# A long convolution's tap stage in row pairs, its transforms on three bank pairs, and a router loop in another order

## The reference, cut to what matters

```
h = sin(f_freq * (z @ f_w1 + f_b1)); h = sin(f_freq * (h @ f_w2 + f_b2)); h = h @ f_w3
h_fwd, h_bwd = h[:, :D] * window, h[:, D:] * window      # window = exp(-t * |delta|), per channel
k = concat([h_fwd, 0, reversed(h_bwd[1:])])              # 2048 taps (latent), 256 taps (context)
y = irfft(rfft(u, 2L) * rfft(k, 2L))[:L] + u * bias
xs = xs + gate1 * ((y * x0) @ out_w)
aff = softmax(modulate(rmsnorm(xs)) @ w_router)
```

## Time and profile before

| what | us |
|---|---|
| median of 3 runs | 4074.03 (4072.95 to 4075.68) |
| the profiled execution | 4073.66 |
| its span | 4071.9 |
| PE busy in the span | 3550.4 (87%) |
| DVE busy | 1823.8 (45%) |
| ACT busy | 1284.7 (32%) |
| long convolution, from PE's first to its last matmul | 461.3 to 886.0 |
| output projection and router, first matmul to last copy of affinities | 908.8 to 1083.6 |

### The profile page before, as it was taken

One profiled execution on the slowest core, in us unless ns is written; L12 is line 12 of the kernel. 1 busy time (PEld: TensorE's weight loads), 2 busy tenths in 40 slices (PEclk: granted clock), 3 DMA queues, 4 the chain that ended last, 5 costly groups with the idle time before them and its releaser, 6 DMA issues. The chain is left out here.

```text
span 4071.9 us, 58678 instructions
## 1 busy us (share of the span) xinstructions
PE 3550.4 (87%) x23807; PEld 2961.4 (73%) x23807; DVE 1823.8 (45%) x2983; ACT 1284.7 (32%) x2029; POOL 434.5 (11%) x411
## 2 busy tenths in 40 slices
PE   4999798978489999997799996759997499999995
PEld 3999543337489999996799996435554499999994
DVE  5233454554533333333402553868886633333332
ACT  4222302013122232333412332236664323233322
POOL 0000000000012121111000111500000012111111
PEclk6999797989689999998899997879998599999997
DMA  6565302044458888884222224886664568878784
GB/s 221 178 206 192 119 0 70 0 138 165 168 201 297 296 294 283 284 297 142 94 88 79 89 67 104 314 315 224 226 221 152 214 233 296 288 276 297 280 294 174
DMA packets 382061, 801.90 MB, mean 197 GB/s; under 512 B 20727, under 2 KB 65468, under 8 KB 380491
## 3 DMA queue, kind: packets, MB, share of 16 engines
q1 hardware_dynamic: 349196, 711.37, 49.4%
q0 software_dynamic: 28368, 86.61, 7.2%
q10 hardware_dynamic: 4368, 2.20, 0.3%
HBM read 691.21 MB, written 108.90 MB: 196 GB/s over the span
## 5 line engine op out<-in xcount | busy, mean ns | idle before, releaser
L1997 PEld LDWEIGHTS moe_banks<-moe_xt,mix_ring 128*128 128x128 f32 x8192 | 1013.3, 191 | 5.5 <-issue 3.2
L1997 PE MATMUL moe_banks<-moe_xt,mix_ring 128*128 128x144 f32 x8192 | 1014.6, 287 | 3.1 <-ACT moe_xt L2032 3.1
L62 PE MATMUL ssdin_banks<-h_leading,ssdin_w_split 128*128 128x384 f32 x1920 | 386.1, 336 | 5.8 <-ACT ssdin_pad L2301 2.9
L2019 PE MATMUL moe_banks<-moe_down_parts,moe_hid_parts 128*128 128x512 f32 x1536 | 357.5, 392 | 0.0
L62 PEld LDWEIGHTS ssdin_banks<-h_leading,ssdin_w_split 128*128 128x128 f32 x1920 | 337.2, 188 | 7.2 <-issue 7.2
L2019 PEld LDWEIGHTS moe_banks<-moe_down_parts,moe_hid_parts 128*128 128x128 f32 x1536 | 285.8, 188 | 71.4 <-issue 13.2
L2077 DVE TENSOR_TENSOR moe_hid<-moe_banks,moe_sg 128x128 f32<-128x128 f32 x256 | 74.6, 292 | 583.3 <-ACT moe_sg L2055 583.3
L2067 DVE TENSOR_TENSOR moe_down_parts<-mix_ring,moe_down_parts 128x2048 fp32r<-128x2048 f32 x128 | 292.2, 2283 | 0.0
L1964 POOL DMA_INDIRECT x_dram<-moe_yc,mix_idx_quarter x128 | 167.5, 1308 | 1090.5 <-DVE moe_yc L2088 1028.2
L2853 PE MATMUL scan_banks<-scan_w,scan_yc 128*128 128x512 f32 x576 | 256.4, 599 | 0.0
L62 PE MATMUL hyin_banks<-h_leading,hyin_w_split 128*128 128x384 f32 x1152 | 238.0, 338 | 11.5 <-DVE hyin_w_split L751 11.5
(11 more groups left out here) (414 smaller groups left out, 4525.4 us busy)
## 6 DMA issues: line engine op xcount, KB each, us to landing
mix_ring<-in_moe_w_gate SPq DMA_DIRECT2D x64, 2048.0 KB, 7.9
mix_ring<-in_moe_w_up SPq DMA_DIRECT2D x64, 2048.0 KB, 12.8
mix_ring<-in_moe_w_down SPq DMA_DIRECT2D x64, 2048.0 KB, 17.2
early_ring<-in_ada_w SPq DMA_DIRECT2D x96, 512.0 KB, 5.8
scan_cum<-row_dram SPq DMA_DIRECT2D x36, 1024.0 KB, 6.4
ssd_w<-in_ssd_in_w SPq DMA_DIRECT2D x10, 2048.0 KB, 9.5
scan_states<-s_dram SPq DMA_DIRECT2D x36, 512.0 KB, 7.9
s_dram<-st_state SPq DMA_DIRECT2D x16, 1024.0 KB, 8.5
```

The lines of the kernel that those rows point to most:

```text
L62: ins = pe.matmul(out(piece), w_at(w[a], k), h_k(h[b], k, piece), start=(k == 0 and a == 0 and b == 0), stop=(k == KD - 1 and a == 1))
L1997: ins = pe.matmul(pb[:, 2 * (f % 2) + j, 0:SLOTS], ring[:, 2 * half + j, k, col:col + P], xt[:, k, :], start=(k == 0), stop=(k == KD - 1))
L2019: ins = pe.matmul(pb[:, LAT_BANK[half], :], hid_parts[:, a, k, :], wd[:, half, b, k, :], start=(k == 0 and a + b == 0), stop=(k == KD - 1 ...
```

## The change: what it does

- Taps: tile order becomes pairs of one forward and one backward tile, (16, 17), (0, 8), (1, 9) to (7, 15). The columns of the features (`zfeat`) are laid out anew so that `filt` has all forward tiles in partitions 0 to 63 and all backward tiles in 64 to 127, and `w3` its two kinds in the same way. The two matmuls of a pair stand next to each other, on the two halves of the array's rows, and write two banks; two such bank pairs (4, 5 and 6, 7) take turns. Pair i waits for both taps of pair i - 2.
- Row corrections: the zero rows come from the window (`negt` is -1e4 there), the bias is a matmul of one row on top of the forward tile of the first two pairs. The four small DVE instructions and `s_edge` are gone.
- DVE forms `zz(4)` to `zz(7)` between the taps, after taps 5, 9, 13 and 17, and `a` after tap 13.
- Transforms: three bank pairs (0-1, 2-3, 4-5). The filter transform's order stays. The input transform takes `U_ORDER` = 8, 2, 0, 3, 1, 4, 5, 6, 7 and starts when its own banks are free. DVE's sums and products follow that order. The first channel group of the inverse waits for what its banks and blocks need in place of all products.
- `phase_hyena_out`: ACT in iteration t does exps t-2, keep_turned t-1, stats t, lead t+2. DVE does top t-2, keep_affinities t-3, soft t-2, residual t, rows t, rest t+2, position t+2. PE's order stays.

```diff
@@ -911,7 +911,15 @@
...
+U_ORDER = (CTX_BLOCK, 2, 0, 3, 1, 4, 5, 6, 7)
...
+PAIRS = (8, 0, 1, 2, 3, 4, 5, 6, 7)
+WITH_ORIGIN = (8, 0)
+def tap_tile(pair, back):
+    return 16 + back if pair == 8 else pair + 8 * back
@@ -921,9 +929,8 @@
...
-        for fold in range(2):
-            sp.dma_start(w3[fold * HY_HID:(fold + 1) * HY_HID, back, :],
-                         io["hy_f_w3"][0][:, back * D + h * HALF:back * D + (h + 1) * HALF]).then_inc(s_half, 16)
+        sp.dma_start(w3[back * HY_HID:(back + 1) * HY_HID, :],
+                     io["hy_f_w3"][0][:, back * D + h * HALF:back * D + (h + 1) * HALF]).then_inc(s_half, 16)
@@ -1004,7 +1010,7 @@
...
-                        sp.wait_ge(s_edge, 1)
+                        sp.wait_ge(s_tap, TAP_TILES)
@@ -1026,15 +1032,25 @@
...
-                def transform(source, ctx_source, counter, emptied, sums, h):
-                    for at, blk in enumerate(ORDER):
-                        lo = 2 + 2 * (at % 2)
-                        if at >= 2:
-                            pe.wait_ge(emptied, h * BLOCKS + (at - 1))
-                        if at in (1, 3, 5):
-                            pe.wait_ge(sums, h * 3 + (at + 1) // 2)
+                def filter_free(at, h):
+                    if at >= 3:
+                        pe.wait_ge(s_ke, h * BLOCKS + (at - 2))
+                    if at in (1, 3, 5):
+                        pe.wait_ge(s_zk, h * 3 + (at + 1) // 2)
+                def input_free(at, h):
+                    if at < 3:
+                        pe.wait_ge(s_ke, h * BLOCKS + (7 + at))
+                    else:
+                        pe.wait_ge(s_pr, h * BLOCKS + (at - 2))
+                    if at in (1, 2, 5):
+                        pe.wait_ge(s_zu, h * 3 + (1, 2, 5).index(at) + 1)
+                def transform(order, source, ctx_source, counter, free, h):
+                    for at, blk in enumerate(order):
+                        lo = 2 * (at % 3)
+                        free(at, h)
@@ -1054,23 +1070,27 @@
...
-                    pe.wait_ge(s_half, h * 96 + 96)
+                    pe.wait_ge(s_half, h * 64 + 64)
...
-                    for tt in range(TAP_TILES):
-                        back = 1 if tt in range(8, 16) or tt == 17 else 0
-                        if tt >= 2:
-                            pe.wait_ge(s_tap, h * TAP_TILES + (tt - 1))
-                        fold, col = slice(tt // 9 * HY_HID, (tt // 9 + 1) * HY_HID), tt % 9 * P
-                        pe.matmul(pb[:, tt % 2, :], filt[fold, col:col + P], w3[fold, back, :],
-                                  start=True, stop=True).then_inc(s_kp, 1)
-                    pe.wait_ge(s_edge, h + 1)
+                    for i, pair in enumerate(PAIRS):
+                        if i >= 2:
+                            pe.wait_ge(s_tap, h * TAP_TILES + 2 * (i - 1))
+                        elif i == 1:
+                            pe.wait_ge(s_g, h * CT_HALF)
+                        origin = pair in WITH_ORIGIN
+                        for back in range(2):
+                            rows = slice(back * HY_HID, (back + 1) * HY_HID)
+                            ins = pe.matmul(pb[:, 4 + 2 * (i % 2) + back, :], filt[rows, pair * P:(pair + 1) * P], w3[rows, :],
+                                            start=True, stop=bool(back) or not origin)
+                        if origin:
+                            ins = pe.matmul(pb[:, 4 + 2 * (i % 2), :], keep["ident"][0:1, :], fbias, start=False, stop=True)
+                        ins.then_inc(s_kp, 1)
+                    pe.wait_ge(s_tap, h * TAP_TILES + 2)
...
-                    transform(lambda s, c: z[:, s, c, :], lambda c: taps[:, 16 + c, :], s_kd, s_ke, s_zk, h)
-                    pe.wait_ge(s_ke, h * BLOCKS + BLOCKS)
+                    transform(ORDER, lambda s, c: z[:, s, c, :], lambda c: taps[:, 16 + c, :], s_kd, filter_free, h)
...
-                    transform(lambda s, c: z[:, s, c, :], lambda c: ut[:, 0, :] if c == 0 else None, s_ud, s_pr, s_zu, h)
-                    pe.wait_ge(s_pr, h * BLOCKS + BLOCKS)
+                    transform(U_ORDER, lambda s, c: z[:, s, c, :], lambda c: ut[:, 0, :] if c == 0 else None, s_ud, input_free, h)
@@ -1078,6 +1098,9 @@
...
+                            if ct == 0 and g != 1:
+                                pe.wait_ge(s_pr, h * BLOCKS + (BLOCKS if g else 7))
@@ -1097,14 +1120,15 @@
...
                 with act.Fori(0, 2) as h:
-                    act.wait_ge(s_half, h * 96 + 96)
-                    for tt in range(TAP_TILES):
-                        if tt >= 2:
-                            act.wait_ge(s_tap, h * TAP_TILES + (tt - 1))
-                        act.activation(win[:, tt % 2, :], delta, ACT.Exp, scale=negt[:, tt:tt + 1]).then_inc(s_win, 1)
+                    act.wait_ge(s_half, h * 64 + 64)
+                    for n in range(TAP_TILES):
+                        tt = tap_tile(PAIRS[n // 2], n % 2)
+                        if n >= 2:
+                            act.wait_ge(s_tap, h * TAP_TILES + (n - 1))
+                        act.activation(win[:, n % 2, :], delta, ACT.Exp, scale=negt[:, tt:tt + 1]).then_inc(s_win, 1)
                     for at, blk in enumerate(ORDER):
                         act.wait_ge(s_kd, h * BLOCKS + (at + 1))
-                        act.activation(kf(blk), pb[:, 2 + 2 * (at % 2):4 + 2 * (at % 2), :], ACT.Copy
+                        act.activation(kf(blk), pb[:, 2 * (at % 3):2 * (at % 3) + 2, :], ACT.Copy
                                        ).then_inc(s_ke, 1)
@@ -1128,20 +1152,6 @@
...
                     dve.wait_ge(s_iv, h * CT_HALF)
-                    for tt in range(TAP_TILES):
-                        dve.wait_ge(s_win, h * TAP_TILES + (tt + 1))
-                        dve.wait_ge(s_kp, h * TAP_TILES + (tt + 1))
-                        tt_(taps[:, tt, :], pb[:, tt % 2, :], win[:, tt % 2, :], ALU.mult).then_inc(s_tap, 1)
-                    dve.wait_ge(s_half, h * 96 + 96)
-                    dve.wait_ge(s_tap, h * TAP_TILES + TAP_TILES)
-                    for tt in (8, 17):
-                        step(dve.memset(taps[0:1, tt, :], 0.0))
-                    for tt in (0, 16):
-                        step(tt_(taps[0:1, tt, :], taps[0:1, tt, :], fbias, ALU.add))
-                    done()
-                    dve.memset(tmp[0:1, 0, 0:1], 0.0).then_inc(s_edge, 1)
                     def q(n):
@@ -1149,20 +1159,31 @@
...
-                    dve.wait_ge(s_edge, h + 1)
-                    dve.wait_ge(s_gs, h * 16 * CT_HALF)
-                    for n in range(4):
-                        step(tt_(zz(4 + n), q(n), q(n + 4), ALU.add))
+                    for n in range(TAP_TILES):
+                        i, back = n // 2, n % 2
+                        dve.wait_ge(s_win, h * TAP_TILES + (n + 1))
+                        if back == 0:
+                            dve.wait_ge(s_kp, h * BLOCKS + (i + 1))
+                        tt_(taps[:, tap_tile(PAIRS[i], back), :], pb[:, 4 + 2 * (i % 2) + back, :], win[:, n % 2, :], ALU.mult
+                            ).then_inc(s_tap, 1)
+                        if n in (5, 9, 13, 17):
+                            k = (n - 5) // 4
+                            dve.wait_ge(s_tap, h * TAP_TILES + (n + 1))
+                            if k == 0:
+                                dve.wait_ge(s_gs, h * 16 * CT_HALF)
+                            step(tt_(zz(4 + k), q(k), q(k + 4), ALU.add))
+                        if n == 13:
+                            done()
+                            step(tt_(a, zz(4), zz(6), ALU.add))
...
-                    step(tt_(a, zz(4), zz(6), ALU.add))
...
+                    dve.wait_ge(s_zk, h * 3 + 2)
@@ -1178,16 +1199,15 @@
...
-                    dve.wait_ge(s_zk, h * 3 + 2)
...
+                    step(tt_(zz(2), x(0), x(2), ALU.subtract))
+                    tt_(zz(3), x(3), x(1), ALU.subtract).then_inc(s_zu, 1)
...
-                    step(tt_(zz(2), x(0), x(2), ALU.subtract))
-                    tt_(zz(3), x(3), x(1), ALU.subtract).then_inc(s_zu, 1)
@@ -1198,9 +1218,9 @@
...
-                    for at, blk in enumerate(ORDER):
-                        lo = 2 + 2 * (at % 2)
-                        dve.wait_ge(s_ke, h * BLOCKS + (at + 1))
+                    dve.wait_ge(s_ke, h * BLOCKS + BLOCKS)
+                    for at, blk in enumerate(U_ORDER):
+                        lo = 2 * (at % 3)
@@ -1482,15 +1502,15 @@
...
                 for t in range(TILES + 3):
+                    if 2 <= t <= TILES + 1:
+                        router.exps(act, t - 2)
+                    if 1 <= t <= TILES:
+                        router.keep_turned(act, t - 1)
                     if t < TILES:
...
                         lead(t + 2)
-                    if 1 <= t <= TILES:
-                        router.keep_turned(act, t - 1)
-                    if 2 <= t <= TILES + 1:
-                        router.exps(act, t - 2)
@@ -1573,19 +1593,18 @@
```

(20 more changed lines are left out.)

3 lines of the change are left out of this document (1 added, 2 removed).

## The result

| what | before | after |
|---|---|---|
| median | 4073.49 (4069.42 to 4075.68, 4 runs) | 3976.76 (3975.37 to 3977.53, 4 runs) |
| ratio | | 0.9763, 95% interval 0.9746 to 0.978 |
| profiled execution, its span | 4073.66, 4071.9 | 3977.04, 3975.4 |

Forecast was 3978 in 3964 to 4000. The spans differ by 96.5 us, where the sum had 96.0. The first view is PE's timeline of the changed kernel through the first half of the channels; it answers to the earlier trace rows.

A forecast was written before the change was run, and what follows sets the result against it. PE was taken as the bound in taps (at half clock) and transforms, a three-engine loop in the router. Gains 29.0 + 6.0 + 26.9 + 34.1 = 96.0 us off 4073.66 give 3977.7, forecast 3978, range 3964 to 4000.

The forecast's parts named there:

- Part 1: Taps: matmuls on the two row halves overlap fully, DVE and ACT become the bound, corrections go; 29.0 us gained.
- The forecast with the bias alone: Taps: the one-row bias matmul stands alone and drains; last sums end at 492.6 and 706.8, 1.2 us less gain.
- Part 2: Filter transform: block 0 follows block 8 with no break over 0.5 us, the clock stays high; 6.0 us gained.
- The bound of 0: Filter transform: the other bound of its forecast gain, 0 in place of 6.0 us.
- rival (b): Clock isn't kept, block 0 starts low: 3984 to 3990; opposite, pairs raise it: 3971; 15%, a third of it faster.
- Part 3: Input transform and start of the inverse: PE's waits go, 62.3 us a half; 14.7 and 12.2, together 26.9 us gained.
- Part 4: Router loop: logits find their bank free, iterations fall to PE's own 14.2 us; 34.1 us gained in all.
- the loop that I took for the bound: Router: logits wait 2.70 us for ACT's exps, queued behind stats and lead, those behind DVE's residual, that behind PE's second projection.
- Rival (a): Taps: the row halves don't overlap, gain 2.8 + 7.0 in place of 29.0 us: 3997; chance 12%.
- (c): Router loop stays above PE's 14.2 us through DVE's series work, 16.2 an iteration, 12 less gain: 3990; chance 10%.
- (d): Transforms: full clock not granted once big and small blocks mix without pauses; slower, 4273 if low throughout; chance 2%.
- (e): Reordered transforms do nothing because DVE's products are the bound; excluded but for small blocks, 8 less: 3986; chance 6%.

The follow-up runs named there:

- the faster version: Changed kernel with the input transform's block 8 and 4 filling instructions in the pause before block 0, bias over 64 rows: 3966.96 us, ratio 0.974.

## Why the prediction was right, point by point

- **Part 1, taps: right, 1.5 short.** The halves gained 13.7 and 16.8 where 13.0 and 16.0 were forecast. Two tiles take two slots: the first pair 2.01 us, 2 x 0.855 and 0.3. The four-tap period was forecast at 4.1 and is 4.03, block 0 at 30.5 behind the first matmul (461.3 to 491.8) and is 29.8. The kernel with one row half shows the overlap, the one with the sums last shows that DVE is the bound. The second half is partly luck: the sum kept DVE's unexplained 1.90 at its loop's end in its path, and it went away, 2.0 gained (from the inverse's last matmul to the first tap of the second half 11.3 before, 9.3 after); from that tap to block 0 the forecast was 1.2 too short (24.8, measured 26.0). The order within a pair was wrong: all four instructions start two by two, not in three steps, without effect on the sum.
- **The one-row bias matmul.** I took the middle between hidden and alone. The trace: alone, on the first two pairs of each half, 2.00 us for its two instructions at the low clock (three of the four; the first of the second half ran at the full clock). By the Trainium skill's "TensorEngine Tiling (Array Packing)", Key Properties, a change of tiling mode drains TensorE; the trace agrees in that nothing overlaps the one-row instructions, and the kernel with the bias over 64 rows, where the taps keep one mode, has the overlap back. The forecast with the bias alone (492.6 and 706.8) was no nearer: block 0 started at 492.60, but 29.84 behind the first matmul, where that forecast had 31.3.
- **Part 2, filter transform: the step that failed, 1.5 in place of 6.0.** The step is that block 8 "now follows the last pair, from about 484.5 to 491.5, and block 0 follows with no break over 0.5 us". It rested on block 8 at the low clock. The pairs raised the clock in the taps (1.00 from 475 to 483), so block 8 was done at 487.2, DVE's sums were not earlier for it, and PE paused 5.45 us and lost the clock again. The bound of 0 was nearer. The opposite case of rival (b) had half of this: it saw that pairs may raise the clock, but priced it as time gained in the taps, which DVE bounds. Three kernels show it: in the changed one the low clock is back behind the pause, filling the pause keeps the clock, and the low clock in the taps removes the pause.
- **Part 3: right (27.3 against 26.9).** No wait in the input transform, and none at the inverse. Order and third bank pair each cover what the other leaves; 14.2 of the 27.3 go if both are undone, the remainder being the early start and the inverse's split wait, which I did not part. A third of the gain is clock: behind the breaks of before, 104 instructions took 47.94 and 46.44 us where full clock gives 44.8, and the first 24 of the inverse 13.17 and 12.26 where they now take 10.46, 9.3 us in all.
- **Part 4, router: mechanism half right, size 4.0 short.** The loop falls to PE's own time, but that is 13.63, not 14.2: the iteration of before that I read the earlier trace rows held an unmarked pause (939.28 - 933.42 = 5.86, where the changed kernel has 5.56), and the turned affinities cost 0.02, not 0.2. Six times 0.57 is 3.4; the end behind residual 8 is 0.8 shorter than forecast (16.7, not 17.5), and the start 0.2 longer. And the loop that I took for the bound was not the one that ended last: the second one, through DVE's `soft` and the turn of the affinities, had the same round of 20.29, and its wait was the one that ended last. I had not seen it; the forecast held because the change broke both.
- The errors -4.5, +4.0, +1.5, +0.4 and the -0.9 outside the parts nearly cancel (+0.5 in all); that 3978 is so close to 3976.76 is in part luck. Rival (a) would have been at about 3989 by the run with one row half, not 3997, since slower taps leave no pause before block 0 and the filter transform runs at the full clock. Rivals (c), (d) and (e) did not happen.

## What to carry to other kernels

When a stage gets faster than the engine that feeds the next one, look at what the clock does in the new pause: filling 5 us of waiting with matmuls whose result is thrown away was worth about 4 to 6 us here, and later work moved there, with the wider bias, 8 to 10. When a wait closes a loop of engines, write down every loop that runs through the same queues, and read for each which wait ends last; with two of equal length, an edit that breaks one shows nothing. Of two edits that each hide the same wait, undoing one costs little (5.5 or 2.8 us here) and undoing both much (14.2), so undo both before calling either useless.

## What the hardware did unexpectedly

- 64-row matmuls on one half of the rows left the clock at 0.50 with PE busy 37.94 of 38.00 us (the last 4 of them block 8, on all rows); on both halves it was granted 1.00 while PE was busy 4.37 of 8.00 us.
- The length of a pause alone does not tell whether the clock falls: behind 2.01 us 112 instructions took 48.33, behind 2.00 us (in the faster version) the next 5 us had 0.66. What differs was not settled. Nor does a longer pause cost more: behind 3.79 us the 112 instructions took 50.03, behind 5.45 us 50.91, and behind 7.93 us, in each half of the kernel with the sums last, 50.82 and 49.74.
- ACT loads the table for Exp before it waits for the maximum, so the load isn't in series with it, as I had it:

```profile
962.65 1.28 ACT L1360 ACT_TABLE_LOAD   x1
965.54 0.27 ACT L1360 ACTIVATE hyout_ex<-hyout_banks,hyout_stats 128x16 f32<-128x16 f32 x1 [1.61 <-DVE hyout_stats L1403]
```

- DVE's unexplained 1.90 at its loop's end is gone: L1279 at 651.34 is followed by the first tap at 652.47. It was on the path, for PE waited 7.84 us for that tap before. The kernel with the router's order alone, whose convolution is the old one, has it too (1.79), and none with the new convolution has; no run looked into why.
